# Gates and k products between the modulation tiles, filter constants ahead of x: one edit of a block kernel on one core

## What is computed

```python
def _adaln(cvec, w_mod, b_mod):                       # w_mod (2048, 12288)
    m = jax.nn.silu(cvec) @ w_mod + b_mod
    return jnp.split(m[..., None, :], 6, axis=-1)     # sh_a, sc_a, g_a, sh_f, sc_f, g_f

h = _rmsnorm(s, p['norm_pre_mix']) * (1.0 + sc_a) + sh_a      # latent and context, own modulation
proj = h @ p['w_in']                                          # k | v | q | gates (32 columns) | z | hyena
qkv = jax.nn.silu(_dwconv(proj[..., COL_K:COL_BETA], p['conv_qkv']))
beta, g = _gdn_gates(proj[..., COL_BETA:COL_Z], p['a_log'], p['dt_bias'])
# 8 gated-DeltaNet heads from k, v, q, beta, g; Hyena long convolution with filter(filt_w1..filt_w4) by FFT;
# output projection, second norm and a SwiGLU feed-forward of width 5632
```

## Time and profile before

| | us |
|---|---|
| median of 3 runs | 1757.85 (1756.18 to 1762.84) |
| the profiled execution | 1752.21 |
| its span | 1750.5 |
| PE busy (matmul) | 1668.6 (95%) |
| PE weight loads | 1447.5 (83%) |
| DVE busy | 1155.9 (66%) |
| ACT busy | 731.7 (42%) |

### The profile page before, as it was taken

How to read it: one execution, slowest core, us unless ns; L and a number is a source line. 1 busy time by engine, 2 the same in 40 slices (tenths; PEclk the granted TensorE clock), 3 DMA queues, 4 the chain that set the end, 5 groups by cost and what they waited for, 6 DMA issues and landing times.

```text
span 1750.5 us, 28282 instructions
## 1 busy us (share of the span) xinstructions
PE 1668.6 (95%) x10418; PEld 1447.5 (83%) x10418; DVE 1155.9 (66%) x1694; ACT 731.7 (42%) x1180; POOL 118.6 (7%) x219
## 2 busy tenths in 40 slices
PE   5988899999999999999997999999999999999998
PEld 1246899998988999999997888888888888788786
DVE  3734688787887888677777755555555555655665
ACT  1344453535344453533333644444444444333331
POOL 2000100101011100000000000000000000111110
PEclk9989999999999999999999899999999999999999
DMA  9986343433424343432698045455444446777773
GB/s 354 389 320 214 112 158 122 157 133 128 151 91 164 109 157 123 168 109 85 235 327 328 25 192 192 192 192 192 190 186 186 185 187 217 267 242 246 270 242 101
DMA packets 79049, 334.20 MB, mean 191 GB/s; under 512 B 7962, under 2 KB 20309, under 8 KB 52512
## 3 DMA queue, kind: packets, MB, share of 16 engines
q1 hardware_dynamic: 58080, 257.97, 40.3%
q0 software_dynamic: 20000, 70.35, 11.6%
q10 hardware_dynamic: 864, 4.47, 0.7%
HBM read 328.56 MB, written 4.19 MB: 190 GB/s over the span
## 4 chain that ended last, share of the span: by engine, by line
PE 81%; DMA 7%; DVE 5%; ACT 4%; issue 1%; DVEq 1%; POOL 0%; ACTq 0%; POOLq 0%
PE g L478 9%; PE o L478 9%; PE o L471 7%; PE o L473 7%; PE o L472 7%; PE g L479 5%; PE o L479 4%; DMA w_mod_tile_o<-in_w_mod_t 4%; PE g L562 3%; PE g L557 2%; DVE w_lo L452 2%; PE g L565 2%; PE g L485 2%; PE o L485 2%; PE g L487 2%; PE g L486 2%
## 5 line engine op out<-in xcount | busy, mean ns | idle before, releaser
L452 DVE TENSOR_TENSOR w_lo<-w_raw,w_hi 128x2048 fp32r<-128x2048 f32 (+1 forms) x207 | 465.5, 2249 | 237.8 <-ACT w_hi L446 236.5
L446 ACT CAST w_hi<-w_raw 128x2048 fp32r<-128x2048 f32 (+1 forms) x208 | 390.5, 1878 | 350.6 <-PE o L473 189.6
L471 PE MATMUL o<-h_hi,w_hi 128*128 128x256 f32 (+1 forms) x896 | 299.4, 334 | 0.0
L473 PE MATMUL o<-h_hi,w_lo 128*128 128x256 f32 (+1 forms) x896 | 282.7, 316 | 0.0
L472 PE MATMUL o<-h_lo,w_hi 128*128 128x256 f32 (+1 forms) x896 | 282.5, 315 | 0.0
L478 PE MATMUL g<-h_hi_lo,w_hi 128*128 128x512 f32 x704 | 245.0, 394 | 0.0
L478 PE MATMUL o<-h_hi_lo,w_hi 128*128 128x512 f32 x688 | 240.7, 394 | 1.0 <-DVE h_hi_lo L1927 1.0
L479 PE MATMUL g<-h_hi_lo,w_lo 128*128 128x256 f32 x704 | 195.0, 277 | 0.0
L479 PE MATMUL o<-h_hi_lo,w_lo 128*128 128x256 f32 x688 | 190.7, 277 | 0.0
L473 PEld LDWEIGHTS o<-h_hi,w_lo 128*128 128x128 f32 x896 | 171.4, 191 | 11.5
L471 PEld LDWEIGHTS o<-h_hi,w_hi 128*128 128x128 f32 x896 | 172.0, 192 | 9.7 <-issue 2.5
(11 more groups left out here) (376 smaller groups left out, 2869.9 us busy)
## 6 DMA issues: line engine op xcount, KB each, us to landing
w_raw<-in_w_ff_t SPq DMA_DIRECT2D x88, 1024.0 KB, 6.3
w_raw<-in_w_heads_t SPq DMA_DIRECT2D x56, 1024.0 KB, 4.9
w_mod_raw<-in_w_mod_t SPq DMA_DIRECT2D x32, 1024.0 KB, 9.5
w_raw<-in_w_down_t SPq DMA_DIRECT2D x32, 1024.0 KB, 5.3
w_mod_piece_h<-in_w_mod_t POOLq DMA_DIRECT2D x112, 256.0 KB, 3.6
w_raw<-in_w_out_t SPq DMA_DIRECT2D x16, 1024.0 KB, 8.5
w_mod_tile_o<-in_w_mod_t POOLq DMA_DIRECT2D x16, 1024.0 KB, 9.6
w_mod_piece_d<-in_w_mod_t POOLq DMA_DIRECT2D x64, 256.0 KB, 5.0
```

What stands on the lines that cost most here:

```text
L446: e.copy(whi[p.split[j]][:, :n], raw[p.raw[j]][:, :n]).then_inc(hi_ready, 1)
L452: e.tensor_tensor(wlo[p.split[j]][:, :n], raw[p.raw[j]][:, :n], whi[p.split[j]][:, :n].bitcast(F32), ALU.subtract).then_inc(lo_ready, 1)
L471: e.matmul(o, a, xh, start=first, stop=False)
L473: return e.matmul(o, b, xh, start=False, stop=last)
```

## The change

- **Queue of the filter constants.** `filt_w4`, `hyena_bias`, `c_win` and the two front parts of `c_dft` (about 2 MiB in all) are issued by ACT, ahead of its wait for `c_in` and so ahead of x, and no more by POOL.
- **Slots of the modulation tiles.** Nine instead of six (new ones at 140, 188 and 24 KB), given out by a list, `MOD_SLOT`; the first split slot 1 (slots 2 and 3) is given up after tile 9, slots 0 and 1 after tiles 23 and 24. A tile waits for the use of the last tile in its slot. The new slots lie over `levf`, over the squares of x and over the front's DFT, so tile 12 also waits for `lev_ready`, tile 25 for `scal_ready`, tile 28 for `fl_act` 11. DVE casts `lev` ahead of `filter_sums_dve`.
- **Banks.** From chunk 4 on, even chunks accumulate in G[0] and no more in O[0], where k is to accumulate.
- **Loads.** SP loads GA behind tile 15 and H0's k behind tile 25; v and q follow the last tile. POOL's first load of `w_mod_raw_h` waits for `mod_used` 32 also.
- **PE's order.** Gates row groups 0 to 7 stand between the tiles of chunk 6, two behind each; 8 and 9 behind tile 30, 10 and 11 behind tile 31; then the last `rows_to_columns`, k groups 0 to 11, gates 12 to 15, k 12 to 15. The four `first_chunk` stand behind k, behind v, in the middle of q and behind q; the small gates products stand in v.
- **ACT and DVE** split GA and H0's k earlier, between chunks; the row copy of the extra modulation chunk follows q's tanh.

```diff
-        mraw = [at(f"w_mod_raw{s}", kb, [P, TILE]) for s, kb in enumerate((88, 104, 96, 112, 64, 72))]
+        mraw = [at(f"w_mod_raw{s}", kb, [P, TILE]) for s, kb in enumerate((88, 104, 96, 112, 64, 72, 140, 188, 24))]
+        MOD_SLOT = [0, 1, 2, 3, 4, 5, 0, 1, 2, 3] + [4, 5, 6, 0, 1] * 3 + [7, 5, 6, 8, 7, 5, 6]
...
+        def mod_bank(m):
+
+            return O[1] if m % 2 else O[0] if m < 4 else G[0]
...
-            def gates_part(i):
-                for k in range(4 * i, 4 * i + 4):
+            def gates_part(k0, k1):
+                if k0 == 0:
+                    tile_ready(pe, GA, 0, 0)
+                for k in range(k0, k1):
                     pe.wait_ge(h_lo, k + 1)
...
-            for m in range(6, 8):
-                chunk(m)
+            chunk(6, *(lambda k=k: gates_part(k, k + 2) for k in range(0, 8, 2)))
+            chunk(7, lambda: None, lambda: None, lambda: gates_part(8, 10), lambda: gates_part(10, 12))
             rows_to_columns(7)
-
-
-            tile_ready(pe, GA, 0, 0)
-            for i in range(4):
-                last = gates_part(i)
-            last.then_inc(w_used, 1)
-            head_piece(pe, H0, 0, 0, "k", 0, 8)
+            head_piece(pe, H0, 0, 0, "k", 0, 12)
+            gates_part(12, KT_N).then_inc(w_used, 1)
+            head_piece(pe, H0, 0, 0, "k", 12, KT_N)
             first_chunk(0)
-            head_piece(pe, H0, 0, 0, "k", 8, KT_N)
+            head_piece(pe, H0, 0, 1, "v", 0, 8)
+            gates_pe(pe, 1)
+            head_piece(pe, H0, 0, 1, "v", 8, 12)
+            gates_pe(pe, 3)
+            head_piece(pe, H0, 0, 1, "v", 12, KT_N)
             first_chunk(1)
-            gates_pe(pe, 1)
-            head_piece(pe, H0, 0, 1, "v", 0, 8)
-            gates_pe(pe, 3)
+            head_piece(pe, H0, 0, 2, "q", 0, 8)
             first_chunk(2)
-            head_piece(pe, H0, 0, 1, "v", 8, KT_N)
+            head_piece(pe, H0, 0, 2, "q", 8, KT_N)
             first_chunk(3)
-            head_piece(pe, H0, 0, 2, "q", 0, KT_N)
...
             act.dma_start(sq[:], A["c_sq"]).then_inc(c_in, 16)
+            act.dma_start(fw[:, 3 * FW:3 * FW + 2 * HY_CH], A["filt_w4"]).then_inc(filt_in2, 16)
+            act.dma_start(hb0[:], A["hyena_bias"]).then_inc(filt_in2, 16)
+            act.dma_start(win[:], A["c_win"]).then_inc(filt_in2, 16)
+            act.dma_start(dft_f[:], A["c_dft"][:, 0:2]).then_inc(filt_in2, 16)
...
             rows_evac(4)
+            split_hi(act, GA, 0, 0)
             h_part(1)
             filter_evac(act, 6)
             filter_evac(act, 7)
             rows_evac(5)
+            h_part(2)
             rows_evac(6)
-            h_part(2)
+            split_hi(act, H0, 0, 0)
             rows_evac(7)
-            split_hi(act, GA, 0, 0)
             h_part(3)
-            split_hi(act, H0, 0, 0)
...
+            v.wait_ge(consts_in, 16 * N_CONST)
+            v.tensor_copy(lev[:], levf[:]).then_inc(lev_ready, 1)
             filter_sums_dve(v)
-            v.wait_ge(consts_in, 16 * N_CONST)
-            v.tensor_copy(lev[:], levf[:])
...
             mod_columns(4)
+            split_lo(v, GA, 0, 0)
             h_rest(1)
             mod_columns(5)
             h_scales(2)
+            h_rest(2)
             mod_columns(6)
-            h_rest(2)
+            split_lo(v, H0, 0, 0)
             mod_columns(7)
-            split_lo(v, GA, 0, 0)
             h_scales(3)
             h_rest(3)
-            split_lo(v, H0, 0, 0)
...
             g.wait_ge(lo_ready, 1)
+            g.wait_ge(mod_used, 32)
...
+                s = MOD_SLOT[t]
+                before = [u for u in range(t) if MOD_SLOT[u] == s]
+                if before:
+                    sp.wait_ge(mod_used, before[-1] + 1)
+                if t == 12:
+                    sp.wait_ge(lev_ready, 1)
+                elif t == 25:
+                    sp.wait_ge(scal_ready, 1)
+                elif t == 28:
+                    sp.wait_ge(fl_act, 11)
...
             for t in range(32):
                 mod_load(t)
-            sp.wait_ge(fl_dve, 11)
-            stream(GA)
-            sp.wait_ge(mod_used, 30)
-            stream(H0)
+                if t == 15:
+                    sp.wait_ge(fl_dve, 11)
+                    load(GA, 0, 0)
+                elif t == 25:
+                    sp.wait_ge(mod_used, 21)
+                    load(H0, 0, 0)
+            sp.wait_ge(mod_used, 31)
+            load(H0, 0, 1)
+            load(H0, 0, 2)
```

More of the change, by code:

```diff
@@ L301, in build @@
         xsq_used, xsum_rows = sem("x_sq_used"), sem("x_sum_rows")
-        mod_landed = [sem(f"mod_landed{s}") for s in range(6)]
+        mod_landed = [sem(f"mod_landed{s}") for s in range(len(mraw))]
+        lev_ready = sem("lev_ready")
         mod_used, rows_out, rows_t, mod_cols = sem("mod_tile_used"), sem("mod_rows_out"), sem("mod_rows_t"), sem("mod_cols")
@@ L794, in chunk @@
                     for kk in range(4):
-                        last = pe.matmul(O[m % 2][32 * kk:32 * kk + 32, :], cpad[:, 4 * j + kk],
-                                         mraw[t % 6][:, kk * 512:(kk + 1) * 512], start=(j == 0), stop=(j == 3))
+                        last = pe.matmul(mod_bank(m)[32 * kk:32 * kk + 32, :], cpad[:, 4 * j + kk],
+                                         mraw[s][:, kk * 512:(kk + 1) * 512], start=(j == 0), stop=(j == 3))
                     last.then_inc(mod_used, 1)
@@ L1068, in rows_evac @@
                     act.wait_ge(rows_t, m)
-                act.copy(rows[:], O[m % 2][:, :]).then_inc(rows_out, 1)
+                act.copy(rows[:], mod_bank(m)[:, :]).then_inc(rows_out, 1)
             def h_part(i):
@@ L1179, in first_act @@
                     evac_qkv(H0, 0, t, 0, t, taps[:, 0, 5 * t + 2:5 * t + 3])
-                    if t == 1:
-                        act.wait_ge(rows_t, 8)
-                        act.wait_ge(first_used, 4)
-                        act.copy(rows[:], G[5][:, :]).then_inc(rows_out, 1)
                     conv_tanh(0, t)
@@ L1186, in first_act @@
                         gates_act2()
+                act.wait_ge(rows_t, 8)
+                act.wait_ge(first_used, 4)
+                act.copy(rows[:], G[5][:, :]).then_inc(rows_out, 1)
             def head_act(p, i, j0, g, u):
```

17 lines of the change are left out of this document (7 added, 10 removed).

## The result

The median of 20 runs is 1743.72 us (1735.03 to 1754.73), beside 1757.41 us for the kernel before on the same chip (20 runs, 1746.83 to 1763.02): ratio 0.9925, 95% interval 0.9906 to 0.9944, so by this ratio 13.2 us less. The profiled execution of the changed kernel is the longest of its 20, 1754.73 us with a span of 1753.1. So the front is read from marks in time, and whole times only from the ratios.

A forecast was written before the change was run, and what follows sets the result against it. PE bounds the kernel from the first head, at 179.61 us, so only the front's lead counts: 1.4 + 3.6 + 13.8 - 2.2 - 0.2 = 16.4, taken as 16, giving 1757.85 - 16 = 1741.8 us; range 1735 to 1750.

The forecast's parts named there:

- Opening: Filter constants on ACT's queue ahead of x: the taps' product and what follows start 6.0 us earlier.
- equal turns: DMA queues share the engines equally, so x, behind the constants, lands at about 36.7 us.
- Stream: Modulation tile loads: less starvation against 2 MiB more ahead, one bubble of 0.5; last tile at 108.9, 1.4 us earlier.
- Gates between tiles: Eight gates groups hide between tiles 24 to 28; last landing to k's start takes 3.4 us for 7.0.
- rival "clock": PE's clock falls during tiles 28 to 30 and k runs at 0.43 a step: 3 to 7 us, 1745 to 1749; chance 0.08.
- k to v's start: From k's start to v's start 15.5 us, with a new wait of 0.8 for v's weight: gain 13.8.
- v's start to q's end: 23.7 us for 21.5, with a new wait of 3.7 for the third chunk's load: a loss of 2.2.
- Tail: From q's end to the first head 11.7 us for 11.5, a loss of 0.2; the head starts at 163.2.
- x late: Constants delay x past 42 us, PE wins nothing in the opening, starvation returns: gain 11, 1747; chance 0.20.
- The overlap doesn't happen: Gates parts with late h rows hold up later modulation tiles: gain 3 to 7, 1751 to 1755; chance 0.08.
- the slower case: Tile 12 waits on SP for lev, moving every later tile; 1767 if lev comes at 76 us; chance 0.04.
- its own signs of being wrong: SP waiting on lev or ACT, x after 39, clock 0.50 between 105 and 120, or a head loop returning the lead.

The follow-up runs named there:

- consts_behind_tanh: Changed kernel with the gates weight behind tile 13, the turn behind the next k's first two pieces, filter constants issued after ACT's tanh: ratio 0.9921.
- small_first: Changed kernel with the filter's five small loads moved from POOL to ACT, ahead of the four large ones: ratio 0.9948.
- chunks_early: Changed kernel with the extra modulation chunks one piece of work earlier each and q in one piece: one execution, span 1748.5 us, head at 173.6.
- small_sp: Changed kernel with the five small filter loads issued first by SP instead of POOL: one execution, span 1739.5 us, head at 170.7.
- turn_late: Changed kernel with PE's last turn of extra modulation rows behind the next k's first two pieces: one execution, span 1745.4 us, head at 165.7.
- combo: Changed kernel with small filter loads first on SP, gates weight behind tile 13 and the turn behind the next k's first two pieces: ratio 0.9936.
- no_overlap: Changed kernel with the twelve gates groups behind the last transpose instead of between the modulation tiles: ratio 0.9996.
- after_again: Changed kernel once more, unedited, on another chip: ratio 0.9947 to the kernel before, head at 171.3 us.
- ga_early: Changed kernel with the gates weight loaded behind tile 13 instead of tile 15: one execution, span 1742.2 us, head at 168.9.
- queue_only: Kernel before with only the four filter constants issued by ACT ahead of x: ratio 0.9974.
- after: The changed kernel's first measurement and profile: ratio 0.9925 to the kernel before, head at 174.2 us.

## Why the prediction was right, and where its steps were not

The forecast of 1741.8 us was 1.9 us below the median, and the range held it. By its steps it deserved less. It put the head's start at 163.2; the profile has 174.2, 11.0 us later, and the second one 171.3. The 11.0 divide as follows.

- **Opening.** The failed step is "the filter's small products wait for the first modulation tile anyway". They waited for their own last small load (11.18), and the taps for the MLP's 14.2 us of layers, at 25.40 instead of 22.6: 3.2 us won of 6.0. Of the 2.8 missing, 1.8 are PE's wait for the MLP's last layer, and 1.0 is the second tile's product, which ended at 23.6. consts_behind_tanh shows the cause by taking it away. The equal turns held for x, which landed at 37.2 (36.7 forecast).
- **Stream.** "I find one bubble of 0.5" failed. Five slots in rotation and GA behind tile 15 left the queue at 162 GB/s for 5 us, about 3 us of loss (5 x (1 - 162/420)). The last tile landed at 113.3 for 108.9: **4.4 late**. Of this 2.6 are the bubble beyond the forecast 0.5. Another 1.7 went ahead of it: tiles 6 to 14 landed over 23.9 us for 22.2 at 2.47 a tile, most of it at tile 10, which landed at 53.4, 3.8 us behind tile 9. So the dip at 50 us shrank and did not vanish. The three new waits of SP (lev, scalars, filter) showed nowhere: from 45 to 60 us every window of five has 406 GB/s or more, and from 65 to 110 us 418 or more.
- **Gates between tiles.** Hidden, as forecast, up to tile 29. Behind that the rival "clock" came in: tile 30's product took 1.94 us and the gates' steps 0.43, so that k began 6.2 us after the last landing for 3.4: **2.8 late**. In small_first, chunks_early, small_sp, turn_late and combo the clock stayed up there, and k began 3.5 us after the last landing. So the term was right at full clock. In turn_late, where the last tile landed at 113.1:

```profile
113.28 1.07 PE L808 MATMUL o<-w_mod_raw,c_padded 128*32 128x512 f32 x8
...
116.58 0.48 PE L473 MATMUL o<-h_hi,w_hi 128*128 128x512 f32 x1
```

- **k to v's start.** 15.7 us for 15.5, with the wait for v's low half 0.78 for 0.8: **0.2**. This largest term, 13.8 us, was right, and no_overlap shows what it hangs on.
- **v's start to q's end.** 24.6 us for 23.7, with waits of 2.38 and 1.51 for one of 3.7. The load took 5.1 us, not the median 6.3; what this saved went to a clock of 0.50 from 154.5 to 157.9. **0.9 late**; at full clock it takes 23.0 to 23.2 (after_again, small_first, ga_early, small_sp, turn_late, combo). The estimate of 4.4 us by the fit of the Trainium skill ("DMA: Bandwidth & Descriptors", section "Anatomy of one DMA — SWDGE (gpsimd) path"), which the prediction cited and didn't use, was not reached by any of these loads in any profile: the quickest took 4.88 us (queue_only).
- **Tail.** 14.4 us for 11.7: **2.7 late**. The step "PE's 2.7 us of the next k behind the tables" held no longer at half clock: PE had stood 4.8 us for the row copy, and then took 5.1 us for 2.7. turn_late shows it: with the two pieces in the idle stretch the tail is 10.5.

So 4.4 + 2.8 + 0.2 + 0.9 + 2.7 makes the 11.0. Why was the total right then? In part by luck. The timed gain of 13.2 (9.8 to 16.5) holds the forecast 16 only at its upper edge, and that on the second chip, 9.3 (5.1 to 13.4), doesn't. The heads of the profiles show 5.4 to 9.2; the spans less FF, in which the draws of the later stages are counted too, differ by 5.8 to 13.7. Four profiles can't say more, and which of the draws the other executions had, the runs don't tell. The rival "clock", given 0.08, was part of what happened, and 1745 to 1749 holds the second chip's median; "x late", given 0.20, did not happen in this kernel, and did in small_first and consts_behind_tanh (x at 45.0 and 44.9). "The overlap doesn't happen" and the slower case found no support. Of its own signs of being wrong, one came, a clock of 0.50 between 105 and 120 us; x after 39 us and SP waiting on lev or ACT did not.

## What to carry to other kernels

Find what each early small product really waits for, and cost the small loads by what large ones are in flight beside them: their rows seem to take turns with large packets. Put loads that need no returned slot ahead of the one that does. And where an engine is left waiting by a rearrangement, price what follows at half clock as well: here that took some 6 us (2.8 ahead of k, 1.5 within q and most of the 2.7 in the tail) of a gain of 16.

## What the runs showed of the hardware

- The product that waits for five small loads of 2 to 33 KB started at 5.8 to 6.2 us with nothing large beside them at first, at 10.3 to 11.5 with 2 MiB under way on ACT's queue and the small loads on POOL's, and at 12.5 to 12.9 with them first on ACT's or SP's queue and, among others, 832 KB under way on POOL's.
- The granted clock fell to 0.50 in the front for 3.4 to 13.7 us at a time, during or behind stretches in which PE waited: in after 2.4 us into the wait of 4.8 ahead of the turn, and in some executions beside the last modulation tiles. Under the same code it fell in one run and not in another.
- The same matmul loop at full clock ran at 285 or at 290 matmuls in 50 us, a whole execution long.
